# Attention of a two-layer encoder on one core: two maps joined ahead of V, bias and maximum in one instruction, four weight pieces rounded on another engine

## What is computed

```python
# B: differential attention, two softmax maps to a head
s = einsum('bqhmd,bkhmd->bmhqk', qb, k) * scale + bias
p = masked_softmax(s, mask)
w = p[:, 0] - lam * p[:, 1]
out_b = einsum('bhqk,bkhd->bqhd', w, v)
# A: s * scale, mask, softmax, times V.   C: with a bias by relative distance
# D: s * scale + bias; a sink joins the largest score and the denominator
x = x + heads.reshape(B, S, D_MIX) @ w_out[l]
```

## Time and profile before

| | |
|---|---|
| median of 3 runs | 1592.3 us (1591.59 to 1592.58) |
| profiled execution, its own time | 1590.78 us |
| profiled execution, span | 1589.0 us |
| busy share PE / DVE / ACT / POOL | 99% / 67% / 35% / 41% |
| chain that ended last | PE 93%, DVE 3%, ACT 2% |
| granted TensorE clock, mean | 0.999 |

### The profile page before, as it was taken

One profiled execution on the slowest core, in us unless ns is written; L12 is line 12 of the kernel. 1 busy time (PEld: TensorE's weight loads), 2 busy tenths in 40 slices (PEclk: granted clock), 3 DMA queues, 4 the chain that ended last, 5 costly groups with the idle time before them and its releaser, 6 DMA issues.

```text
span 1589.0 us, 32114 instructions
## 1 busy us (share of the span) xinstructions
PE 1565.9 (99%) x11432; PEld 1531.1 (96%) x11432; DVE 1061.6 (67%) x2523; ACT 555.5 (35%) x1538; POOL 649.7 (41%) x552
## 2 busy tenths in 40 slices
PE   7999999999999999999999999999999999999998
PEld 6888999999999999999978899999999999999998
DVE  4784899688888543444467848996888875434444
ACT  5686522655554000000067766126555530000000
POOL 6616604543555333222175175235333452332321
PEclk9999999999999999999999999999999999999999
DMA  9026288999999999999961252989999999999996
GB/s 364 5 107 265 94 326 329 335 410 409 409 409 410 408 410 410 410 406 408 404 229 66 96 238 95 361 300 379 409 409 409 409 409 409 410 407 405 408 405 255
DMA packets 141942, 525.76 MB, mean 331 GB/s; under 512 B 16160, under 2 KB 19744, under 8 KB 139424
## 3 DMA queue, kind: packets, MB, share of 16 engines
q1 hardware_dynamic: 86336, 322.57, 51.7%
q0 software_dynamic: 55520, 202.14, 32.4%
HBM read 523.60 MB, written 1.05 MB: 330 GB/s over the span
## 4 chain that ended last, share of the span: by engine, by line
PE 93%; DVE 3%; ACT 2%; issue 1%; POOL 1%; DMA 0%; SPq 0%; DVEq 0%; ACTq 0%
PE ps L604 90%; PE ps L601 2%; DMA x<-in_x 0%; DVE grid L1423 0%; DVE negmax L1427 0%; ACT grid L297 0%; ACT grid L982 0%; ACT wh L1018 0%; ACT grid L1081 0%; POOL wl L572 0%; ACT fhl L1004 0%; ACT grid L968 0%; DVE x L1485 0%; POOL wl L566 0%; DVE gqm L1309 0%
## 5 line engine op out<-in xcount | busy, mean ns | idle before, releaser
L604 PE MATMUL ps<-grid,ring 128*128 128x160 f32 (+1 forms) x3712 | 520.3, 299 | 0.0
L604 PE MATMUL ps<-grid,nat 128*128 128x160 f32 (+1 forms) x3712 | 520.3, 299 | 0.0
L604 PEld LDWEIGHTS ps<-grid,ring 128*128 128x128 f32 x3712 | 508.6, 190 | 0.0
L604 PEld LDWEIGHTS ps<-grid,nat 128*128 128x128 f32 x3712 | 508.6, 190 | 0.0
L1714 DVE SCALAR_TENSOR_TENSOR grid<-grid,amount 128x1024 f32<-128x1024 f32 x96 | 123.3, 1284 | 155.3 <-DMA grid<-in_peer_v,lists 155.2
L1714 DVE SCALAR_TENSOR_TENSOR grid<-gath_a,amount,grid 128x1024 f32<-128x1024 f32 x94 | 120.7, 1284 | 143.4 <-DMA gath_a<-in_peer_v,lists 143.2
L566 POOL TENSOR_TENSOR wl<-grid,wh 128x512 fp32r<-128x512 f32 (+2 forms) x128 | 142.2, 1142 | 144.3 <-ACT wh L1018 128.0
L586 POOL DMA_INDIRECT gath_a<-in_u_rows,lists x96 | 121.7, 1268 | 184.9 <-DVE dots L1683 132.2
L586 POOL DMA_INDIRECT gath_a<-in_peer_v,lists x96 | 103.1, 1074 | 203.1 <-DVE grid L1714 66.6
L586 POOL DMA_INDIRECT grid<-in_peer_v,lists x96 | 98.4, 1025 | 195.2 <-DVE grid L1714 70.8
L1018 ACT ACTIVATE wh<-grid 128x512 fp32r<-128x512 f32 (+2 forms) x128 | 67.8, 575 | 311.5 <-DMA grid<-in_w_in 273.4
(11 more groups left out here) (202 smaller groups left out, 1737.5 us busy)
## 6 DMA issues: line engine op xcount, KB each, us to landing
nat<-in_peer_v SPq DMA_DIRECT2D x128, 512.0 KB, 11.4
ring<-in_peer_v SPq DMA_DIRECT2D x128, 512.0 KB, 11.6
nat<-in_peer_u SPq DMA_DIRECT2D x104, 512.0 KB, 7.6
ring<-in_peer_u SPq DMA_DIRECT2D x104, 512.0 KB, 7.5
grid<-in_peer_u SPq DMA_DIRECT2D x48, 512.0 KB, 6.1
grid<-in_peer_wq SPq DMA_DIRECT2D x8, 2048.0 KB, 10.3
grid<-in_w_out SPq DMA_DIRECT2D x2, 4096.0 KB, 12.4
grid<-in_w_in SPq DMA_DIRECT2D x3, 2048.0 KB, 15.9
```

The costliest lines, as they stand in the source:

```text
L604: return nc.tensor.matmul(dst, a, b, start=first, stop=last)
```

## The change

Three edits.

1. The scale of the scores moves into the queries: B, C and D through `gqm`, A through the scale of the eviction copy. Scaling, bias and largest score become one `tensor_tensor_reduce` for each map: it writes minus (score + bias), and its accumulator takes the minimum. The exponential is then taken with scale -1. The semaphore `sc_read` goes; `score(g)` waits for `negmax_ready` in its place.
2. For B the two maps are joined before V: a new function `join(g)` on VectorE runs at the start of step g + 2, ahead of `biased`. It takes the reciprocals, forms -lambda * sum1 / sum2 and replaces each head's first map by map1 + that * map2, in place. `turn` and `mix` of a B group then handle one map to a head: two transposes in place of four, half of the products with V, a copy of 256 columns, and one scaling in `mixed`. A new semaphore `joined` is waited for by `turn`.
3. The first four pieces of the output weights are rounded by VectorE, at the end of steps 7 to 10, with a semaphore of their own (`w_first`), which GpSimd and TensorE wait for.

```diff
+NFIRST = 4
...
                         if g >= 3:
-                            pe.wait_ge(sc_read, past[sc_read] + g - 2)
+                            pe.wait_ge(negmax_ready, past[negmax_ready] + g - 2)
...
                         pe.wait_ge(probs_ready, past[probs_ready] + g + 1)
+                        if kind == "B":
+                            pe.wait_ge(joined, past[joined] + joins.index(g) + 1)
...
-                        for i in range(4):
-                            ins = tr(ps[:, 3 + g % 3, i * P:(i + 1) * P], probs[:, g % 3, i * P:(i + 1) * P])
+                        for i, c in enumerate(c for cs, _ in blocks(g) for c in cs):
+                            ins = tr(ps[:, 3 + g % 3, i * P:(i + 1) * P], probs[:, g % 3, c:c + P])
...
-                        if NG0 + 1 < i < NG0 + 6:
-                            high_pieces(NPI + i - NG0 - 2, NPI + i - NG0 - 1)
...
-                    high_pieces(NPI + 4, len(pieces))
+                    high_pieces(NPI + NFIRST, len(pieces))
...
-                    for a, b, c in ((0, 4, 5), (4, 12, 3), (12, 16, 7)):
-                        ins = v.tensor_scalar(gqm[:, a:b], rowmask[:, a:b], gcol[:, c:c + 1], None, ALU.mult)
+                    for a, b, c, kind in ((0, 4, 5, "C"), (4, 12, 3, "B"), (12, 16, 7, "D")):
+                        ins = v.tensor_scalar(gqm[:, a:b], rowmask[:, a:b], gcol[:, c:c + 1], SCALE[kind], ALU.mult, ALU.mult)
...
-                            ins = v.scalar_tensor_tensor(out=dst[:, a:e].rearrange("p (h k) -> p h k", k=n), in0=src[:, a:e].rearrange("p (h k) -> p h k", k=n),
-                                                         scalar=SCALE[kind], in1=bv, op0=ALU.mult, op1=ALU.add)
-                        ins.then_inc(sc_read, 1)
-                        dve.wait_ge(sc_read, past[sc_read] + g + 1)
-                        red = v.tensor_reduce(negmax[:, b4, 0:m], dst.rearrange("p (h k) -> p h k", k=n), X, ALU.max, negate=True)
+                        for i, (_, _, _, j) in enumerate(ms_):
+                            row = 12 if kind == "A" else BROW[kind] + j
+                            red = v.tensor_tensor_reduce(out=dst[:, i * n:(i + 1) * n], in0=src[:, i * n:(i + 1) * n], in1=bias[:, row, k0:], scale=-1.0,
+                                                         scalar=3e38, op0=ALU.add, op1=ALU.min, accum_out=negmax[:, b4, i:i + 1])
...
+                    def join(g):
+                        kind, tt, ms_ = groups[g]
+                        n, b, b3, m = P * (tt + 1), g % 4, g % 3, len(ms_)
+                        dve.wait_ge(probs_ready, past[probs_ready] + g + 1)
                         ch.step(v.reciprocal(rinv[:, b, 0:m], rsum[:, b, 0:m]))
...
+                        r2, s2 = (w[:, b, 0:m].rearrange("p (h m) -> p h m", m=2) for w in (rinv, rsum))
+                        ch.step(v.scalar_tensor_tensor(out=r2[:, :, 1], in0=r2[:, :, 1], scalar=lamt[:, 5:6], in1=s2[:, :, 0], op0=ALU.mult, op1=ALU.mult))
+                        for i in range(0, m, 2):
+                            one, two = (probs[:, b3, c * n:(c + 1) * n] for c in (i, i + 1))
+                            ins = v.scalar_tensor_tensor(out=one, in0=two, scalar=rinv[:, b, i + 1:i + 2], in1=one, op0=ALU.mult, op1=ALU.add)
+                        ins.then_inc(joined, 1)
...
                     for i in range(NG + 3):
+                        if i - 2 in joins:
+                            join(i - 2)
                         if i < NG:
                             biased(i)
...
+                        if NG0 + 1 < i < NG0 + 2 + NFIRST:
+                            n = NPI + i - NG0 - 2
+                            dve.wait_ge(ld_wout, past[ld_wout] + 16)
+                            dve.wait_ge(w_used, past[w_used] + n - 3)
+                            src, w = pieces[n]
+                            v.tensor_copy(wh4[:, n % 4, 0:w], src).then_inc(w_first, 1)
```

More of the change, by code:

```diff
@@ L386, in build, with blocks @@
         NG = len(groups)
+        joins = [g for g in range(NG) if groups[g][0] == "B"]
+        def blocks(g):
+            kind, tt, ms_ = groups[g]
+            step = 2 if kind == "B" else 1
+            return [([(i * (tt + 1) + kb) * P for kb in range(tt + 1)], ms_[i][3]) for i in range(0, len(ms_), step)]
+        PER_LAYER = {}
+        for count, which in (
+                (1, "rms_ready gqm_ready cqt_done cqt_ready qka_ready prepped lists_ready best_shift "
+                 "wexp_ready lists_t listt_ready acts_ready rs0_ready yt_cleared diag_ready rs_spread rs_kept"),
+                (2, "kr_ready up_done up_copied lam_ready y_turned mean_ready root_ready "
+                 "heads_ready heads0_ready yt_act yt_dve"),
+                (3, "osq_ready k_evicted y_chunk"),
+                (4, "hn_ready rs_used ht_done"),
+                (NFIRST, "w_first"),
+                (7, "q_evicted"),
+                (sum(g[0] == "B" for g in groups), "joined"),
+                (8, "xsq_done xt_done hsq_ready sq_used x_ready xf_ready"),
+                (10, "tr_done"),
+                (NB // OCT, "ones_ready"),
+                (3, "picked"),
+                (12, "h_ready"),
+                (15, "sc_done negmax_ready probs_ready pt_done pt_ready pv_done o_ready"),
+                (16, "ld_bias ld_wout ld_wq0 ld_wq1 ld_wq2 ld_wq3 qp_done qst_ready ks_done sraw_ready sq_kept wq_high "
+                 "wq_rest gain_in"),
+                (24, "fh_ready fl_ready"),
+                (32, "ld_up"),
+                (NG4, "hots_ready hota_act gate_done"),
+                (NG4 + 2, "gated"),
+                (64, "w_rest w_used"),
+                (64 - NFIRST, "w_high"),
+                (NB, "gelu_used"),
+                ((GT - 1) * NG4, "dist_ready"),
+                (NK, "prod_done act_stored y_done"),
+                (2 * NR, "gath_used"),
+                (32 * NR // OCT, " ".join(f"gath_in{b}" for b in range(OCT))),
+                (16 * (USES + NO), " ".join(f"nat_in{s}" for s in range(OCT))),
+                (32, " ".join(f"spare_in{e}" for e in range(NE)))):
+            for which_ in which.split():
+                PER_LAYER[which_] = count
         class Chain:
@@ L749, in mix @@
                         pe.wait_ge(pt_ready, past[pt_ready] + g + 1)
-                        for i in range(len(ms_)):
-                            v = vcols(kind, ms_[i][3])
+                        for i, (cs, head) in enumerate(blocks(g)):
+                            v = vcols(kind, head)
                             for kb in range(tt + 1):
@@ L1088, in turned @@
                             act.wait_ge(pv_done, past[pv_done] + g - 1)
-                        A(pt[g % 2], ps[:, 3 + g % 3, :], ACT.Copy).then_inc(pt_ready, 1)
+                        w = P * sum(len(cs) for cs, _ in blocks(g))
+                        A(pt[g % 2][:, 0:w], ps[:, 3 + g % 3, 0:w], ACT.Copy).then_inc(pt_ready, 1)
                     def root_of(src, dst, n):
@@ new lines, in mixed @@
+                        if kind == "B":
+                            h0, m, by = 4 + ms_[0][3], m // 2, rinv[:, b, 0:m].rearrange("p (h m) -> p h m", m=2)[:, :, 0]
+                        else:
+                            h0, by = HROW[kind] + ms_[0][3], rinv[:, b, 0:m]
+                            ch.step(v.reciprocal(by, rsum[:, b, 0:m]))
+                        v.tensor_tensor(oall[:, tt, h0:h0 + m, :], ps[:, 6 + g % 2, 0:m * HD].rearrange("p (h d) -> p h d", d=HD),
+                                        over(by, 2, HD), ALU.mult).then_inc(o_ready, 1)
```

73 lines of the change are left out of this document (14 added, 59 removed).

## The result

| | before | changed |
|---|---|---|
| median, 6 runs each | 1591.94 us (1590.18 to 1594.84) | 1603.88 us (1598.60 to 1606.94) |
| ratio | | 1.0073, 95% interval 1.0062 to 1.0085 |
| profiled execution, span | 1589.0 us | 1596.8 us |
| its own time and mean granted clock | 1590.78 us, 0.999 | 1598.60 us, 1.000 |

The change is slower, as forecast, but by 11.9 us and not by 6: 1603.9 us lies 0.4 above the range. The profiled execution is the quickest of the six changed ones, and the only one with a mean granted clock of 1.000. The others have 0.990 to 0.997.

A forecast was written before the change was run, and what follows sets the result against it. TensorE, busy 99% of the span, was taken to bound the kernel, almost balanced with VectorE in attention. Held joins cost +3.0 us a layer, +6.0 on 1590.8 gives 1596.8, and 1598.3 us on the median; range 1591.0 to 1603.5.

The forecast's parts named there:

- the joins wait for GpSimd's subtraction: Attention steps 8 to 10: VectorE's two-SBUF-input join operations wait for a whole subtraction; +3.0 us a layer, chance 0.59.
- lower bound: Join's one-column lambda factor in steps 8 to 10: if not held, each round 0.26 us shorter, +2.2 us a layer.
- joins not held: Rival for the attention loop: 256-column joins run beside the subtraction, rounds about 2.1 us, 1591.7 us in all; chance 0.19.
- TensorE's saving comes through: Rival: six groups 0.64 us shorter on TensorE, a layer could be 3.8 us shorter, 1584.6 us; chance 0.12.
- second case: Earlier trace: three tiny scalings of gqm take 2.84 us under four subtractions, given as evidence that two-SBUF-input operations wait.
- Rounds of 3.2 us: Attention steps 8 to 10, from one rounding copy's end to the next: 3.2 us, three rounds ending at 103.6 us.
- two handovers: In a round, with half transpose (0.24) and half product (0.43), they lead from the join's end at +1.88 to +2.63 us.
- TensorE's clock falls: Rival: half-busy TensorE in the rounds drops to half rate, +2.5 to +6 us more a layer; chance 0.10.
- The likeliest case: Held joins with no clock fall: +3.0 us a layer, 1598.3 us, bounds 1596.7 to 1599.9; chance 0.59.
- from 82.01 to about 82.9: First layer, start of turn(1): delayed because join(1) needs group 1's exponentials; halved transposes and products give it back by turn(2).
- The holes of 1.6 us: TensorE idle gaps ahead of turn(6), turn(7) and turn(8), expected to be 1.6 us each in the rounds.
- The rival's price: TensorE at half rate from the second round to turn(11) or the loop's end: 1603.3 to 1610 us; chance 0.10.

The follow-up runs named there:

- e2: Changed kernel with GpSimd's first four subtractions of the output weights held back until all six joins are done: 1596.78 us, ratio 1.0034 to the kernel before.
- e13: Changed kernel with one line moved: join(i-1) behind biased(i) in step i, instead of join(i-2) ahead of it: 1591.28 us, ratio 0.9998 to the kernel before.
- e8: Kernel before with edit 3 alone (four pieces rounded by VectorE): 1590.33 us, ratio 0.9997.
- e10: Changed kernel with rounding back on ScalarE, GpSimd's first four subtractions after the joins, eleven identity products ahead of turn(1): 1591.06 us, ratio 1.0000 to the kernel before.
- e9: Changed kernel with seven identity products in each of steps 8 to 10 and eleven ahead of turn(1): 1597.17 us, ratio 1.0039 to the kernel before.
- e4: Changed kernel with seven identity products on TensorE ahead of the transposes in each of steps 8, 9 and 10: 1599.69 us, ratio 1.0055 to the kernel before.
- e1: Changed kernel run again without an edit, for its spread and a second profile: 1604.06 us, ratio 1.0078 to the kernel before.
- e12: Kernel before with edit 1, joins for groups 5 to 8 only, placed behind biased, ScalarE rounding, GpSimd's first four subtractions after the joins: 1586.54 us, ratio 0.9974.
- e11: Changed kernel with GpSimd's first four subtractions after the joins and eleven identity products ahead of turn(1): 1592.03 us, ratio 1.0007 to the kernel before.

## Why the prediction was right and where it was wrong

**Right.** That the joins wait for GpSimd's subtraction, on TensorE's path, and that this makes the change slower. e2 takes the subtraction away and the round falls from 3.37 to 2.35 us; e13 moves the join and it falls alike. The question behind the lower bound ("the rows show no operation that short beside a subtraction") is settled: one column is held as 64 are, 1.25 us. So far the Trainium skill's rule (SBUF — State Buffer, Who interferes with whom) and the rows agree, and so does e8: an operation with one input from PSUM runs beside the subtraction. The new instruction reads 0.28 and 0.42 us with its accumulator read hidden, and the copy 0.42, as costed. The rival "joins not held" is refuted by the 1.25 us, "TensorE's saving comes through" by e10: even with no subtraction near, TensorE waits for the joins. One reading doesn't carry what was put on it: the "second case", the scalings of gqm, is a TENSOR_SCALAR with one tensor input and a scalar from SBUF, of the kind of L1447, which wasn't held. Its 2.84 us and the held copy of e13 show that some operations with one SBUF tensor are held as well; which ones, no run here settles. The forecast doesn't need the second case, since the held sums of the earlier trace rows carry it.

**Mis-sized.** "Rounds of 3.2 us" are 3.37. Up to the join's end the sum was right: the 256-column sum takes 0.48 us and not 0.42, but the lambda factor ends 0.02 us behind GpSimd and not 0.08, so the join ends 1.86 us after the copy (1.88 in the forecast). The "two handovers" were too small, 0.08 us in all: turn(6) starts 0.11 us behind the join, and the scaling starts 2.81 us after the copy's end in place of 2.63. Three rounds make 0.5 us, about the difference between the forecast's +3.0 and the measured +3.5 a layer. Of the 3.5, by the rounds of e2 (2.35 us), 3 x 1.02 = 3.1 us are the wait for the subtraction; the other 0.4 are what e2, without that wait, still loses in its first layer.

**Wrong.** The step that failed is "*TensorE's clock falls* ... I give this a small chance", at 0.10, on the ground that "the holes of a round are shorter" than the idle time at the end of the program. The likeliest case therefore had no clock term. It happened in ten of the eleven executions of the changed kernel, to judge by their mean clock. The error has two parts. The sum moved turn(1) "from 82.01 to about 82.9" (it came 1.2 later, counted from the stage's start) and took the delay as given back by turn(2); it did not look at what TensorE does meanwhile. TensorE is through with score(3) 0.2 us sooner, and the hole grew from 1.13 to 2.51 us. And I measured the risk by whether a hole is as long as the only idle stretch seen before a fall. The holes of 1.6 us were right for turn(7) and turn(8) (1.65), but turn(6) has 2.07, and it was behind 2.07 and 2.51 us that the clock fell, not every time but in most executions. e9 is the test: both holes filled with idle products, 1597.2 us and a clock of 0.999 to 1.000 in all runs; e4, with one filled, still shows falls at the other.

The two losses add up: 7.0 us for the joins in the stages of two layers (e9, at full clock, is +6.2 in time), and the rest, 5 to 7 us, for the clock. The rival's price, 1603.3 to 1610 us, holds the measured 1603.9, but in part by luck: it had the fall in steps 8 to 11 of both layers, and not behind turn(1), and in e1's profile nearly all of the clock's cost lies in one layer. The Trainium skill's page TensorE: Matmul & The Clock Gate, Part 1, which says that an idle engine drops to half of the pulses, was cited and given too little weight; these traces agree with it in the two levels, 0.50 behind those holes and 1.00 elsewhere.

What stays open: why a fall follows a hole in one execution and not in the next. And e10's stage is 0.4 us shorter than before, where the sum of steps had 1.3; the difference is not traced to a single wait. Its late subtractions hold another operation in turn, the sink's largest score (L1450 there, two SBUF inputs), for 1.17 and 0.85 us in place of 0.16.

## What to carry to other kernels

When an operation is moved to another engine, look at what stands behind it on both sides: here the consumer's reaction (GpSimd starting to subtract) met exactly the next two-input operation of VectorE. Put operations with an input from PSUM behind such a handover, which kept their usual time beside a subtraction in e8 and e13 (a copy with its one input in SBUF did not), or let the helper engine start later when its result has time.

A shortened step on TensorE, ahead of a wait that stays, makes a longer hole. List the holes of the new schedule, not only its end, and compare them with holes behind which the clock fell (2.07 and 2.51 us here) and those behind which it held (1.13 us). Fill such a hole, or keep it short. One profile at full clock proves nothing about the median.

## What the runs showed of the hardware

- An operation of VectorE with two SBUF inputs waits for a running GpSimd subtraction even if it has one column (1.25 us in place of 0.22). One with an input from PSUM doesn't (0.68 us beside it). A copy of 512 columns with its one input in SBUF was held as well (e13: 0.90 us in place of 0.42).
- The granted clock went to 0.50 behind holes of 2.51 and 2.07 us of TensorE (e1, second layer) and stayed there for nearly 7 and some 10 us, though in the first stretch TensorE was busy from 874.7 on without a break. Behind a hole of 1.13 us it stayed at 1.00 in the profiles of the kernel before, edit 1, edit 3 and e12, and these three changed kernels have a mean clock of 0.999 to 1.000 in all executions.
- With 128 x 128 products of the identity in both holes (e9) or in the one ahead of turn(1) and the subtractions late (e10, e11), the mean clock was 0.999 to 1.000 in all 27 executions.
- The joined bias, mask and minimum instruction costs 0.28 us at 128 columns and 0.42 at 256 with an input from PSUM, 0.21 and 0.34 from start to start.
